# The u projection of an S5 layer: weights as the stationary operand, and a way to the states through DRAM

## The reference, cut to what matters

```
h = rms_norm(x, norm_mix_g);  u = h @ w_in[:, u columns]      # (1056, 1024)
ug = u.reshape(B, L, 64 groups, 16 channels)
bu = einsum('blgc,gpc->blgp', ug, b_bar)      # complex
state[t] = lambda * state[t-1] + bu[t]        # scan over tokens
y = einsum('blgp,gcp->blgc', state, c) + d_skip * ug
```

## Time and profile before

| | |
|---|---|
| median of three runs | 4053.01 us (4045.92 to 4063.34) |
| span of the profiled execution, first to last instruction | 4050.0 us |
| TensorE (PE) busy | 85% |
| VectorE (DVE) busy | 75% |
| ScalarE (ACT) busy | 39% |
| GpSimd (POOL) busy | 27% |
| mean granted TensorE clock | 0.918 of 2.4 GHz |
| mean DMA rate | 324 GB/s |

### The profile page before, as it was taken

The page is one execution under the profiler, slowest core; times in us unless marked ns, Lnnn a source line. Parts: engine busy times, 40 slices in busy tenths (PEclk is TensorE's granted clock), DMA queues, the critical chain, the costliest instruction groups (busy, mean ns, idle before and its releaser), DMA issues. The chain is left out here.

```text
span 4050.0 us, 48497 instructions
## 1 busy us (share of the span) xinstructions
PE 3454.9 (85%) x15934; PEld 2301.5 (57%) x15934; DVE 3038.4 (75%) x5871; ACT 1574.1 (39%) x3898; POOL 1085.6 (27%) x880
## 2 busy tenths in 40 slices
PE   8989998987778679888677858876869999999999
PEld 6757876544544445355466644444436666666666
DVE  6584113888988778899776889899858887877775
ACT  2223421525753234376533323325752323323232
POOL 0100001332223343322222233332323333333331
PEclk9989998998988889998888878897989999999999
DMA  3023457998879999988798989886999999999996
GB/s 143 8 79 127 139 185 268 389 417 324 298 297 416 354 404 408 394 281 281 295 366 330 372 332 405 332 327 238 391 387 406 416 415 416 416 417 414 399 413 260
DMA packets 296284, 1311.90 MB, mean 324 GB/s; under 512 B 39458, under 2 KB 99330, under 8 KB 189666
## 3 DMA queue, kind: packets, MB, share of 16 engines
q0 software_dynamic: 120320, 854.80, 53.4%
q1 hardware_dynamic: 175330, 453.87, 29.6%
q10 hardware_dynamic: 384, 0.13, 0.0%
HBM read 1250.07 MB, written 56.79 MB: 323 GB/s over the span
## 5 line engine op out<-in xcount | busy, mean ns | idle before, releaser
L1034 POOL DMA_INDIRECT arena<-in_uv,arena x800 | 1029.6, 1287 | 2271.8 <-DVE arena L1183 2019.3
L726 PE MATMUL ps<-arena 128*128 128x256 f32 (+2 forms) x3456 | 1108.7, 480 | 150.3 <-DMA arena<-in_w_stat 74.0
L1173 DVE CUSTOM_DVE_ANT_0 arena<-arena 128x1024 f32<-128x1024 f32 x800 | 974.2, 1220 | 48.4 <-DMA arena<-in_uv,arena 41.1
L1183 DVE SCALAR_TENSOR_TENSOR arena<-arena 128x1024 f32<-128x1024 f32 x736 | 943.3, 1282 | 72.3 <-ACT arena L1273 71.9
L726 PEld LDWEIGHTS ps<-arena 128*128 128x128 f32 x3456 | 675.9, 199 | 538.9 <-issue 310.1
L1264 ACT ACTIVATE arena<-arena 128x2 f32<-128x2 f32 x400 | 81.1, 203 | 1174.6 <-DVE arena L1173 1156.0
L2652 PE MATMUL ps<-arena 128*128 128x256 f32 x2048 | 468.1, 382 | 0.0
L2661 PE MATMUL ps<-arena 128*128 128x512 f32 x1024 | 460.1, 592 | 0.1
L2652 PEld LDWEIGHTS ps<-arena 128*128 128x128 f32 x2048 | 383.1, 192 | 48.1 <-issue 0.5
L2661 PEld LDWEIGHTS ps<-arena 128*128 128x128 f32 x1024 | 194.4, 190 | 191.9 <-issue 185.5
L2777 DVE TENSOR_TENSOR arena<-arena 128x256 f32<-128x256 f32 x128 | 79.8, 623 | 259.0 <-ACT arena L2742 161.6
(11 more groups left out here) (296 smaller groups left out, 4118.8 us busy)
## 6 DMA issues: line engine op xcount, KB each, us to landing
arena<-in_uv SPq DMA_DIRECT2D x256, 512.0 KB
arena<-in_w_stat SPq DMA_DIRECT2D x216, 512.0 KB
arena<-in_cache_k SPq DMA_DIRECT2D x64, 512.0 KB
arena<-in_cache_v SPq DMA_DIRECT2D x64, 512.0 KB
arena<-in_w_mov SPq DMA_DIRECT2D x14, 2048.0 KB, 14.9
scr_w<-arena SPq DMA_DIRECT2D x8, 2048.0 KB, 24.3
arena<-scr_w SPq DMA_DIRECT2D x16, 1024.0 KB
arena<-in_uv,arena POOLq DMA_INDIRECT x800
```

The lines of the kernel that those rows point to most:

```text
L726: last = nc.tensor.matmul(ps[:, bank, 0:w], wbuf[m % NWB][:, kc * P:(kc + 1) * P], moving[:, kc, :], start=(kc == 0), stop=(kc == KC - 1))
L1034: pool.indirect_dma_start(ring[s % RING], None, dr["uv"], bass.IndirectOffsetOnAxis(ap=idx[:, g % 4, j:j + 1], axis=0)).then_inc(row_in[s ...
L1173: nc.vector.tensor_tensor_reduce(ring[s % RING][:, 0:D], ring[s % RING][:, 0:D], h2r[:, b % 2, :], 1.0, 0.0, ALU.mult, ALU.add, act_in[:, ...
L1183: nc.vector.scalar_tensor_tensor(accr[:, b % 2, :], ring[s % RING][:, D:2 * D], wgt[:, s % RING:s % RING + 1], accr[:, b % 2, :], ALU.mult ...
```

## The change

u is now made in 8 tiles of 128 channels. The stationary operand is a 128 by 128 block of weights, and the moving operand is 512 tokens of `hT`, twice per tile. The sample tokens are made in front of the last tile, with 64 more matmuls that move 32 columns each. ScalarE stores each tile as [channel, token in chunk, chunk] in `u_st`, and SP writes it to DRAM (`scr_u`). When the last matmul is done, SP issues 20 loads that fill `ug` from DRAM. There are 8 for the first 48 groups (one per token in the chunk, 16 partitions each), 4 for the samples, and 8 for the other 16 groups. The transposes of u on TensorE and their copies are gone, as are the small sample matmuls. The wait for the loads stands in block 3, in front of the first pair's matmuls, and for the last 16 groups in front of pair 24. GpSimd zeroes all of `m_toe` at the start of block 2.

```diff
@@ sync
-                sp.wait_ge(u_free, ST8 + 2)
-                sp.dma_start(scr_us, us_st[0:NS, :]).then_inc(us_out, 16)
+                for j in range(KC):
+                    if j == KC - 1:
+                        samples_out()
+                    sp.wait_ge(u_free, 2 * j + 2)
+                    sp.dma_start(scr_u[j * P:(j + 1) * P], u_st[:, j % 2]).then_inc(u_out[j % 2], 16)
+                sp.wait_ge(u_ready, 2 * KC)
+                sp.wait_ge(spill, 16)
+                sp.wait_ge(ug_zero, 1)
                 sp.wait_ge(us_out, 16)
-                for t in range(NNEW):
-                    sp.dma_start(us_tok[0:NSEQ, :, t, :], ...).then_inc(us_in, 16)
+                for k in range(2):
+                    for m in range(2):
+                        sp.wait_ge(u_out[m], 16 * (3 + k))
+                    gs = slice(0, G_EARLY) if k == 0 else slice(G_EARLY, G)
+                    for t in range(ST8):
+                        sp.dma_start(ug[CH * t:CH * (t + 1), gs, 0:P], scr_u.rearrange("(g c) t n -> t c g n", c=CH)[t, :, gs]
+                                     ).then_inc(ug_in[k], 16)
+                    for t in range(NNEW * (1 - k)):
+                        sp.dma_start(ug[64 + CH * t:64 + CH * (t + 1), :, P:NUG],
+                                     scr_us.rearrange("(g c) t q -> t c g q", c=CH)[t]).then_inc(us_in, 16)
                 sp.wait_ge(k_d, 2)
@@ tensor
-                        for kc in range(KC):
-                            last = nc.tensor.matmul(ps[0:rows, n % 4, :], tok, slab[:, k, kc, :], ...)
+                def samples():
+                    for j in range(KC):
                         for kc in range(KC):
+                            last = nc.tensor.matmul(ps[:, 4, j * NS:(j + 1) * NS], slab_cols(j, kc), hT[:, kc, SEQ:T], ...)
+                for j in range(KC):
+                    if j >= 2:
+                        pe.wait_ge(u_free, 2 * (j - 1))
+                    if j == KC - 1:
+                        samples()
+                    for half in range(2):
+                        for kc in range(KC):
+                            last = nc.tensor.matmul(ps[:, 2 * (j % 2) + half, :], slab_cols(j, kc), hT[:, kc, 512 * half:512 * (half + 1)], ...)
-                for q in range(G // 4): ... nc.tensor.transpose(... u_tok[:, g], ident[:, :])
-                for g in range(G): ... nc.tensor.matmul(ps[64:P, 7, ...], us_tok[0:NSEQ, g]..., ident[0:NSEQ, 0:NSEQ])
@@ scalar
+                        nc.scalar.activation(u_st[:, j % 2, :, 64 * half:64 * (half + 1)].rearrange("p t n -> p n t"),
+                                             ps[:, 2 * (j % 2) + half, :].rearrange("p (n t) -> p n t", t=ST8), ACT.Copy).then_inc(u_free, 1)
@@ block 3, tensor
+                    if gp == 0:
+                        pe.wait_ge(us_in, 16 * NNEW)
+                        pe.wait_ge(ug_in[0], 16 * ST8)
+                    if 2 * gp == G_EARLY:
+                        pe.wait_ge(ug_in[1], 16 * ST8)
```

More of the change, by code:

```diff
@@ L251, in hybrid_step @@
         pw = lay(AT_PW, [9, 2, GP])
-        u_tok = lay(AT_TOE, [G, ST8, CH])
-        us_tok = lay(AT_HH, [G, NNEW, CH])
-        us_st = lay(AT_HH, [D])
+        u_st, us_st = lay(AT_HH, [2, ST8, P]), lay(AT_HH + 2 * D, [KC, NNEW, NSEQ])
         bri = lay(AT_HH + 4096, [2, GP, CH])
@@ L271, in hybrid_step @@
         u_ready, u_free = sem("u_ready"), sem("u_free")
-        ug_ready, ug_free = sem("ug_ready"), sem("ug_free")
+        u_out, ug_in = [sem(f"u_out{k}") for k in range(2)], [sem(f"ug_in{k}") for k in range(2)]
+        us_ready, us_taken = sem("us_ready"), sem("us_taken")
         par_a, par_v, spill = sem("par_a"), sem("par_v"), sem("spill")
-        scr_us = nc.dram_tensor("scr_us", (NS, D), F32, kind="Internal").ap()
+        scr_u = nc.dram_tensor("scr_u", (D, ST8, P), F32, kind="Internal").ap()
+        scr_us = nc.dram_tensor("scr_us", (D, NNEW, NSEQ), F32, kind="Internal").ap()
+        G_EARLY = 6 * P // CH
         us_out, us_in = sem("us_out"), sem("us_in")
         k_ready, k_free, k_d, cl_ready = sem("k_ready"), sem("k_free"), sem("k_d"), sem("cl_ready")
-        toe_zero, toe_in, low_zero = sem("toe_zero"), sem("toe_in"), sem("low_zero")
-        NU = 2 * ST8 + 2
-        U_STEPS = (ST8, *range(ST8))
+        toe_zero, toe_in, ug_zero = sem("toe_zero"), sem("toe_in"), sem("ug_zero")
         def complex_step(dve, mul, re, im, ar, ai, br, bi, sign, t):
@@ L303, in _, with samples_out @@
                 sp.dma_start(scr_h, hT.rearrange("p c t -> p (c t)")).then_inc(spill, 16)
[L304 to L309 removed]
+                def samples_out():
+                    sp.wait_ge(us_taken, 1)
+                    sp.dma_start(scr_us.rearrange("(c p) t q -> p c (t q)", p=P), us_st.rearrange("p c t q -> p c (t q)")
+                                 ).then_inc(us_out, 16)
+                for j in range(KC):
[6 more added lines that the diff above has]
+                sp.wait_ge(ug_zero, 1)
+                sp.wait_ge(us_out, 16)
+                for k in range(2):
[8 more added lines that the diff above has]
+                                     scr_us.rearrange("(g c) t q -> t c g q", c=CH)[t]).then_inc(us_in, 16)
                 sp.wait_ge(k_d, 2)
@@ L313, in _ @@
             def _(pool):
+                nc.gpsimd.memset(m_toe[0:32], 0.0).then_inc(toe_zero, 1)
+                nc.gpsimd.memset(m_toe[32:64], 0.0).then_inc(toe_zero, 1)
+                nc.gpsimd.memset(m_toe[64:P], 0.0).then_inc(toe_zero, 1)
+                pool.wait_ge(toe_zero, 3)
                 pool.wait_ge(spill, 16)
-                pool.wait_ge(u_ready, NU)
-                nc.gpsimd.memset(ug[0:64, :, P:NUG], 0.0).then_inc(toe_zero, 1)
-                pool.wait_ge(ug_ready, G // 4)
@@ L318, in _, with slab_cols @@
-                pool.wait_ge(toe_zero, 1)
-                nc.gpsimd.memset(m_toe[32:64], 0.0)
-                nc.gpsimd.memset(m_toe[64:P], 0.0).then_inc(toe_zero, 1)
+                pool.wait_ge(u_ready, 2 * KC)
+                nc.gpsimd.memset(ug[0:64, :, P:NUG], 0.0).then_inc(ug_zero, 1)
             @block.tensor
             def _(pe):
[L324 to L330, removed]
-                        for kc in range(KC):
-                            tok = hT[:, kc, s:SEQ:ST8] if s < ST8 else hT[:, kc, SEQ:T]
-                            last = nc.tensor.matmul(ps[0:rows, n % 4, :], tok, slab[:, k, kc, :],
+                def slab_cols(j, kc):
+                    return slab[:, j // 4, kc, (j % 4) * P:(j % 4 + 1) * P]
@@ new lines, in samples @@
+                def samples():
+                    for j in range(KC):
+                        for kc in range(KC):
+                            last = nc.tensor.matmul(ps[:, 4, j * NS:(j + 1) * NS], slab_cols(j, kc), hT[:, kc, SEQ:T],
+                                                    start=(kc == 0), stop=(kc == KC - 1))
+                    last.then_inc(us_ready, 1)
+                for j in range(KC):
+                    pe.wait_ge(slab_in[j // 4], 16)
+                    if j >= 2:
[4 more added lines that the diff above has]
+                        for kc in range(KC):
+                            last = nc.tensor.matmul(ps[:, 2 * (j % 2) + half, :], slab_cols(j, kc), hT[:, kc, 512 * half:512 * (half + 1)],
@@ L334, in _ @@
                                                     start=(kc == 0), stop=(kc == KC - 1))
                         last.then_inc(u_ready, 1)
[L336 to L345, removed]
+                pe.wait_ge(u_free, 2 * KC)
@@ L358, in _ @@
                     last.then_inc(k_ready, 1)
[L359 to L363, removed]
             @block.scalar
@@ L373, in _ @@
                 nc.scalar.activation(r2, r2, ACT.Sin).then_inc(par_a, 1)
[L374 to L388, removed]
+                for j in range(KC):
+                    if j >= 2:
+                        act.wait_ge(u_out[j % 2], 16 * (j // 2))
+                    if j == KC - 1:
+                        act.wait_ge(us_ready, 1)
+                        nc.scalar.activation(us_st.rearrange("p c t q -> p c q t"),
+                                             ps[:, 4, 0:KC * NS].rearrange("p (c q t) -> p c q t", c=KC, t=NNEW), ACT.Copy).then_inc(us_taken, 1)
+                    for half in range(2):
+                        act.wait_ge(u_ready, 2 * j + half + 1)
+                        nc.scalar.activation(u_st[:, j % 2, :, 64 * half:64 * (half + 1)].rearrange("p t n -> p n t"),
+                                             ps[:, 2 * (j % 2) + half, :].rearrange("p (n t) -> p n t", t=ST8), ACT.Copy).then_inc(u_free, 1)
+                act.wait_ge(toe_zero, 3)
                 for q in range(G // 8):
@@ L467, in _ @@
                                  pw[:, 8, 0, :], pw[:, 8, 1, :], 1, tmp[:, :, 0])
-                dve.wait_ge(ug_ready, G // 4)
-                for k in range(4):
-                    nc.vector.memset(m_toe[0:32, k * G // 4:(k + 1) * G // 4, :], 0.0).then_inc(low_zero, 1)
```

7 lines of the change are left out of this document (2 added, 5 removed).

## The result

The changed kernel takes 4073.47 us in the median of 21 runs (4052.55 to 4088.63). The kernel before, run beside it, takes 4051.44 (21 runs). The ratio is 1.0048 with a 95% interval of 1.0035 to 1.0060, so the change costs 14 to 24 us.

A forecast was written before the change was run, and what follows sets the result against it. TensorE's own list was taken to pace the kernel up to S, then S itself. S shifts +15.1 us, a longer slow start adds 1.3, giving 4066.4 profiled; the median lies 3.0 higher: 4069 us, range 4046 to 4092 (8 in 10).

The forecast's parts named there:

- What the page and the windows said: Whole kernel: TensorE's own list sets the pace in 160 to 197 us; a shift of S reaches the end in full.
- S: Start of the states' first matmul on TensorE, which VectorE's scan hangs on; forecast to move from 197.7 to 212.8 us.
- Projection and samples: TensorE before the loads: projection saves 13.7 us, samples take 22.5 at a falling clock, last tile loses 2.5; end at 172.5.
- clock term: Samples and last tile on TensorE: with the clock held at 1.00, the projection would end 10.3 us sooner, at 162.2.
- The rival in which the clock holds: Samples on TensorE keep clock 1.00; projection ends at 162.2, 10.3 us sooner, time 4059 us; chance 13%.
- Rate of the loads: Early loads of u from DRAM, 16 partitions each: 3.15 MB at 97 GB/s take 32.4 us.
- The rival in which the DMA engines pace the loads: Loads of u run at 323 GB/s, 9.7 us for 32.4; time 4048 us; chance 15% with its edge.
- Sample loads: Loads of the samples from DRAM before S: 4096 pieces of 32 bytes cost 4 to 12 us, taken as 4.
- the rival of dearer loads: Loads before S: 32-byte pieces +8, SP less far ahead up to +10.8, or 75 GB/s +9.6; 4077 to 4088; chance 22%.
- SP as second gate: Block 2 ends only when SP has issued all 20 loads, about 212; S needs 1.4 us more, so 213.
- Behind S: After S: 1.3 us for a longer slow start; 4 us of new TensorE wait at L538, covered by 12.68 us of slack.
- The second rival with the clock held: DMA engines pace the loads and the samples keep clock 1.00; TensorE's convolution kernels then gate S; time 4041 us.

The follow-up runs named there:

- spread samples: Changed kernel with each tile's 8 sample matmuls in front of its 16 large ones, not all 64 before the last tile: 4065.02 us, ratio 1.0022.
- short gate: Changed kernel with samples by tile and 128-partition loads; sample loads first, only 16 groups awaited before S, 48 loaded from block 3: 4038.74 us, ratio 0.9965.
- wide layout: Changed kernel with u in DRAM by group, 8 stores per tile; with loads filling 128 partitions 4050.07 us, ratio 0.9997; with 16-partition loads 4064.37 us.

## Why the prediction was right, step by step

- **What the page and the windows said.** That the pace is set by TensorE's own list up to S, and by S afterwards, held. The shift of S reached the end in six kernels, as far as intervals 10 to 15 us wide can tell.
- **Projection and samples.** Forecast end 172.5, measured 171.6. The samples took 21.97 us for 22.5, with the clock at 0.50 as taken, and the last tile lost 2.3 for 2.5 (16.26 us for 13.98). The spread samples confirm the price by another way: 14.3 us at full clock for the 14.7 worked out from decode attention, and 8.35 us of S for a clock term of 10.3. The rival in which the clock holds is out.
- **Last copy.** Taken as 1.0, measured 1.03, against 0.60 before. The first load left SP at 173.27 for 173.9.
- **Rate of the loads.** This is the term that decided, and its size was a little off: 109 GB/s for 97, so 28.9 us for 32.4 by the same sum. The mechanism is shown by three widths of one and the same data: 112 GB/s into 16 partitions, 191 into 32, 311 into 128. The rival in which the DMA engines pace the loads named the size of the effect well (323 GB/s) and its cause wrongly. Pieces of 512 bytes do come near that rate (311), but only over all partitions. The 226 GB/s that the forecast took for 32 partitions stood on a window of 0.2 us; these loads ran at 179 to 191. The Trainium skill ("SBUF — State Buffer", Door 1: The DMA port swizzle) gives 104, 189 and 328 GB/s for these three widths at 1 MiB a transfer, and the windows here agree within 8%.
- **Sample loads.** Taken as 4 us, measured as 4.5: by the sum's own terms the early loads of u have landed at about 204.6 (173.27 + 2.5 + 28.9), and the last sample load lands near 209. The start-up of 2.5 us was not measured by itself. The 4 was partly luck: the earlier trace rows give 3.5 us for half as many pieces, so 7 by count, and 4 only if the share of 0.55 there is taken as filled up. Of the rival of dearer loads only SP's part came, with about 2.5 us of its 10.8.
- **SP as second gate.** Forecast at 212 and within a microsecond of the data. It came at 210.8, 1.7 us behind the data, and cost about 2.5 us of S. Two errors of opposite sign thus met: the faster loads took 3.5 us off, the gate gave part of that back. S was forecast at 212.8 and came at 212.04, and that it came so near is luck.
- **Behind S.** The 1.3 us for a longer slow start at low clock were not there: from S to the scan are 17.07 us, 17.03 before. Such a term does exist: it was 1.5 us in the short gate, behind 2.9 us of idling and not behind a long one. So the scan starts at 229.1, not 231. The 4 us of new wait at L538's successor don't show either; the slack at L803 is whole. In front of the states I had forecast 22 to 25 us of idling with a DMA as releaser. It was 16.1 us with the block change as releaser, since the convolution kernels ran until 194.7 instead of 188.
- **The time.** The sum was 4066.4 for the profiled execution; it was 4065.2 by the span. That match is partly luck, since the profiled run was 6.5 us faster than the median. The median came out at 4073.47 for 4069. By the ratio the change cost 19.5 us, where S moved 14.4; both fit the interval, and whether the 5 us between them are noise is open. The forecast leaned to "within 0.5%" and had 0.37 on slower; the median lies right at that bound.
- **One rival's time.** The second rival with the clock held was put at 4041; by its own terms it is 4048 less the 10.3 us of the clock, 4038. It changes nothing above.

What the change was worth is now a sum of measured parts. By these parts, the new projection at full clock and without a way back through DRAM would start S near 182 (190.26 - 8.35), an estimate that the short gate, whose loads are hidden, bears out with 180.92. Low clock costs 8.35 us and the loads 21.8, of which 18.7 come from filling 16 partitions at a time.

## What to carry to other kernels

A layout change through DRAM has a narrow and a wide side. Put the narrow pieces (few partitions for each transfer) on the side that lies beside other work, and let the side that is waited for fill all 128 partitions: the same bytes here took 30 us or 12. Small matmuls in one long run lowered TensorE's granted clock here, and the large ones behind them paid too; spread among the large ones they cost two thirds. And a block ends only when SP has issued all its transfers, so loads that are needed late belong to the next block (about 2.5 us here).

## What was not expected

- **A hole in TensorE's list.** In the changed kernel TensorE stood 5.21 us between two convolution kernels with nothing to wait for. It is in two other kernels as well: the one with the spread samples (5.41) and the one with the late loads moved (5.27). It is in none of the others. In the changed kernel one packet of the instruction queue shows beside the loads in that stretch (183 to 190 us; packets, MB, share of the engines):
```profile
q1 hardware_dynamic: 1473, 0.74, 122.1%
q8 instruction: 1, 0.02, 1.6%
```
  The traces say more. In the seven kernels without the hole (the kernel before among them) the first such packet moves about 4 to 6 us after the convolution kernels start. In the three with it, it moves 12 to 13 us after (185 to 186 us here), inside the hole. These three are the only ones in which loads into 16 partitions are queued from the start of the convolution kernels; with 16-partition loads in the wide layout the first load leaves SP at 176.6, 3.9 us later, and the packet is through at 177 to 178. So it fits all ten traces that TensorE's next instructions came late behind the queued loads. The profile doesn't say whose instructions a packet holds, so this stays short of shown. It cost S nothing here, since S waited for the loads anyway.
- **Strided copies.** ScalarE's copy of 128x512 with a write stride of 512 bytes takes 1.03 to 1.09 us in all 16 copies, and 0.60 before. The last eight:
```profile
L395 ACT ACTIVATE arena<-ps x8: 1031/1066/1083, 99.5 to 171.6; 128x512 f32<-128x512 f32 x8
```
- **32 partitions below a doubling.** Twice the partitions gave 179 to 191 GB/s and not twice 112.
